# ScalarE's start reordered and PE's warm-up cut from seven products to five in a hybrid decoder step

## What is computed

```
for l in range(DEPTH):
    hn = rmsnorm(xp, norm_mix[l])
    q_nope, q_rope, c_kv, k_r, qb, kb, vb, g = project_in(hn, pos_p, w_in[l], ...)
    a_out, b_out, c_out = MLA, dilated-window attention, conformer convolution
    xp = xp + concat[a_out, b_out, c_out] @ w_out[l]
    xp = xp + peer(rmsnorm(xp, norm_ffn[l]), ...)      # top-16 product-key retrieval over 16384 experts
    ... the same for the 8 sample tokens, with their caches
y = rmsnorm(x, norm_final)
```

## Time and profile before

| what | value |
|---|---|
| median of 3 runs (lowest to highest) | 2046.28 us (2045.88 to 2046.68) |
| the profiled execution's own time | 2044.14 us |
| its span, first to last instruction | 2042.3 us |
| PE busy | 2016.6 us (99%) |
| PEld, DVE, ACT, POOL busy | 88%, 76%, 63%, 6% |
| mean granted TensorE clock | 0.998 |
| first product of the first chunk (L940) starts | 14.97 us |

### The profile page before, as it was taken

How to read it: one execution, slowest core, us unless ns; L and a number is a source line. 1 busy time by engine, 2 the same in 40 slices (tenths; PEclk the granted TensorE clock), 3 DMA queues, 4 the chain that set the end, 5 groups by cost and what they waited for, 6 DMA issues and landing times. The chain is left out here.

```text
span 2042.3 us, 40772 instructions
## 1 busy us (share of the span) xinstructions
PE 2016.6 (99%) x15562; PEld 1796.2 (88%) x15562; DVE 1550.3 (76%) x3543; ACT 1290.1 (63%) x2567; POOL 123.2 (6%) x140
## 2 busy tenths in 40 slices
PE   9999999999999999999999999999999999999998
PEld 7876999999999888788887779999999998887887
DVE  6846699868899776676678467989589997765766
ACT  5466455668888656565564654565688886555654
POOL 2200000000000100100022000000000001001000
PEclk9999999999999999999999999999999999999999
DMA  9454367776666898898763642777766669988886
GB/s 331 143 174 165 125 202 255 244 249 218 212 221 212 294 318 292 296 325 272 242 231 143 214 158 91 241 252 252 237 217 223 211 219 309 312 281 296 271 267 219
DMA packets 137376, 481.76 MB, mean 236 GB/s; under 512 B 25666, under 2 KB 42082, under 8 KB 130768
## 3 DMA queue, kind: packets, MB, share of 16 engines
q1 hardware_dynamic: 124640, 438.45, 64.2%
q0 software_dynamic: 10496, 40.42, 5.6%
q10 hardware_dynamic: 2048, 0.30, 0.1%
HBM read 475.83 MB, written 104.21 MB: 284 GB/s over the span
## 5 line engine op out<-in xcount | busy, mean ns | idle before, releaser
L2235 DVE TENSOR_TENSOR parts<-region,parts 128x1024 fp32r<-128x1024 f32 x512 | 625.6, 1222 | 300.1 <-ACT parts L1563 297.9
L1239 PE MATMUL ps<-tokens_hi,parts 128*128 128x256 f32 x4096 | 760.5, 284 | 0.0
L1563 ACT CAST parts<-region 128x1024 fp32r<-128x1024 f32 x512 | 538.8, 1052 | 270.5 <-PE ps L1286 202.4
L1286 PE MATMUL ps<-parts,parts_hw 128*128 128x512 f32 x3024 | 688.7, 390 | 0.0
L1286 PEld LDWEIGHTS ps<-parts,parts_hw 128*128 128x128 f32 x3024 | 567.0, 188 | 123.8 <-DVE parts_hw L2285 6.9
L1239 PEld LDWEIGHTS ps<-tokens_hi,parts 128*128 128x128 f32 x4096 | 637.0, 188 | 0.9 <-issue 0.4
L1239 PE MATMUL ps<-parts_hw,parts 128*128 128x256 f32 x2048 | 574.1, 280 | 0.0
L1239 PEld LDWEIGHTS ps<-parts_hw,parts 128*128 128x128 f32 x2048 | 386.7, 189 | 0.0
L1609 ACT ACTIVATE big<-ps 128x256 f32<-128x256 f32 (+31 forms) x252 | 131.7, 522 | 146.8 <-PE ps L1239 146.8
L1597 ACT CAST parts_hw<-big 128x256 fp32r<-128x256 f32 x256 | 171.4, 670 | 0.7 <-DVE big L2296 0.7
L1590 ACT ACTIVATE region<-region 128x128 f16<-128x128 f16 x512 | 169.3, 436 | 0.0
(11 more groups left out here) (329 smaller groups left out, 2199.5 us busy)
## 6 DMA issues: line engine op xcount, KB each, us to landing
region<-in_peer_uT SPq DMA_DIRECT2D x256, 512.0 KB, 4.0
region<-in_peer_v SPq DMA_DIRECT2D x256, 512.0 KB, 4.8
out<-in_state_win_k SPq DMA_DIRECT2D x112, 384.0 KB, 4.9
out<-in_state_win_v SPq DMA_DIRECT2D x112, 384.0 KB, 4.9
big<-in_window_keysT SPq DMA_DIRECT2D x16, 576.0 KB, 5.3
big<-in_state_win_v SPq DMA_DIRECT2D x48, 192.0 KB, 4.0
region<-in_w_out SPq DMA_DIRECT2D x4, 2048.0 KB, 8.9
big<-in_peer_wq SPq DMA_DIRECT2D x4, 2048.0 KB, 11.4
```

What stands on the lines that cost most here:

```text
L1239: mm = pe.matmul(ps[:, j % ZB, 0:SEQ], a, hp[b][:, c, :], start=(c == 0 and n == 0), stop=(c == KD - 1 and n == 2))
L1286: mm = pe.matmul(ps[:, 2 * half + t, :], w_t[a][:, 128 * t:128 * t + 128], v_t[b][:, 512 * half:512 * half + 512], start=(j == 0 and n == ...
L1563: act.copy(hi_t[n % HIGHS], rows_t[n % ROWS]).then_inc(high[l], 1)
L2235: dve.tensor_tensor(lo_t[n % ROWS], rows_t[n % ROWS], hi_t[n % HIGHS], ALU.subtract).then_inc(low[l], 1)
```

## The change

ACT's six constant DMAs move from behind the `norm_mix` gains to behind the three roots of the first norm; the table load and its throwaway root thereby follow the gains directly. WARM goes from 7 to 5. Nothing else changes; no wait is added or taken away.

```
-WARM = 7
+WARM = 5
...
-            act.dma_start(iota[:, :], C["iota"]).then_inc(consts_ld, 16)
...
-            act.dma_start(wmask[:, :], C["wmask"]).then_inc(consts_ld, 16)
             act.wait_ge(ones_set, 1)
             act.activation(stat[:, 15:16], stat[:, 15:16], ACT.Sqrt)
...
                     root(0, MIX, 1)
+                    act.dma_start(iota[:, :], C["iota"]).then_inc(consts_ld, 16)
...
+                    act.dma_start(wmask[:, :], C["wmask"]).then_inc(consts_ld, 16)
```

More of the change, by code:

```diff
@@ L1358, in _ @@
                 act.dma_start(g_mix, L("norm_mix", 0).rearrange("(k p) -> p k", p=P)).then_inc(gm_ld[0], 16)
[L1359 to L1364, removed]
             act.wait_ge(ones_set, 1)
@@ L1378, in _ @@
                     root(0, MIX, 1)
+                    act.dma_start(iota[:, :], C["iota"]).then_inc(consts_ld, 16)
+                    act.dma_start(pages[:, :], A["page_rows"]).then_inc(consts_ld, 16)
+                    act.dma_start(sub[:, :], C["sub"]).then_inc(consts_ld, 16)
+                    act.dma_start(rope[:, :, :], C["rope"]).then_inc(consts_ld, 16)
+                    act.dma_start(bmask[:, :], C["bmask"]).then_inc(consts_ld, 16)
+                    act.dma_start(wmask[:, :], C["wmask"]).then_inc(consts_ld, 16)
                 def input_high(c, k):
```

## The result

The changed kernel takes 2051.13 us (median of 9 runs, 2049.97 to 2053.05) against 2046.27 for the kernel before (9 runs beside it). It is slower by 4.86 us: ratio 1.0025, 95% interval 1.0017 to 1.0034. The forecast was 2045.1, with 2047.6 as the upper end. The sign was wrong, and the time lies outside the range.

The account below looks back on a forecast made before the run. PE, busy 99% of the span, was taken to be the bound, so its start mattered: L902 at 18.7 instead of 19.90, set by the constants landing at 14.6, gains 1.2 us: 2046.28 - 1.2 = 2045.1, range 2043.6 to 2047.6.

Parts of the forecast that it names:

- The table and the roots: ACT and DVE start: table load at 1.65, reciprocal 2.39 us earlier, from the second square on DVE 1.71 us earlier.
- Two products fewer: PE warm-up: four fast passes of 0.43 go, 1.72 us; PE is free to transpose at 9.52 instead of 11.24.
- The six issues in their new place: ACT behind the third root: issues take 3.50 us, first eviction at 11.95, costing 0.44 of the 1.72 gained.
- The rival that ACT is held in its issues: ACT's issues held up like SP's `q_norm`: first eviction about 14.5, 1.3 us later, 2047.6; chance 0.06.
- When the constants land: PE's wait before the first L940: `iota` lands near 10.75, five more at 0.77 each, the last at 14.6.
- the sum: Eviction chain lets L902 go at 18.62, PE's own way at 18.7: 1.2 us earlier, median 2045.1.
- The rule that was weighed there: DMA engines take turns among queue rows with work; constants would pass w_in's backlog, a gain of 1.2 us.
- The rival: Constants land late, PE waits before the first L940: 2048.5, or 2050.2 with the clock; chance 0.09, a fifth with clock.
- its threshold of 16.0: Landing of the constants at which nothing is left of the gain: 15.9 + 4.02 is L902's old 19.90.
- the forecast's four signs of being wrong: `wmask` after 16; an ACTq issue of 2 us or more; clock falling before 20 us; later PE wait growing by the gain.
- the forecast's comparison: PE's idling from 13.07 to 14.7 is shorter than the 1.8 us it sat through before.

Follow-up runs that it names:

- the kernel with the second chunk held back: Changed kernel, but SP issues the eight pieces of w_in's second chunk only behind the third root: 2048.31 against 2046.10 for before (ratio 1.0007).
- POOL's first: First constant in the changed kernel with POOL issuing the six constants from its own queue instead of ACT: 2044.77 against 2046.10 for before (ratio 0.9990).
- both experiments that idled for 2.9 us or more: Changed kernel with a warm-up of seven, 2051.41; changed kernel with SP issuing w_in's second chunk only behind the third root, 2048.31.
- the one that was taken apart: Changed kernel, 2051.13; against it, 16 idle products on PE ahead of the wait for the constants gave 2048.31.
- the kernel with the wait at its use: Changed kernel, but PE waits for the six constants in layer 0's second norm, not before the first chunk: 2043.53 against 2045.92; repeated, 2044.70 against 2045.84.

## Why the prediction was wrong

**The table and the roots: right.** Third root at 8.25 (forecast 8.35), second square at 6.98 and released by X (forecast 7.1).

**Two products fewer: right in kind, and hidden in this execution.** The first transpose began at 10.68, not at 9.52, because the clock rose later than in the execution before: loads of PEld in the changed kernel take 0.33 us as late as 8.52 and 0.20 from 9.38, where the earlier trace rows has 0.34 at 6.68 and 0.19 at 7.38.

```profile
8.52 0.33 PEld L915 LDWEIGHTS ps<-ident,ones 128*128 128x128 f32 x1 [0.52 <-issue]
...
9.38 0.20 PEld L915 LDWEIGHTS ps<-ident,ones 128*128 128x128 f32 x1 [0.52 <-issue]
```

The forecast took the clock's rise of one execution for that of all. It costs up to 1.2 us here and decided nothing.

**The six issues in their new place: too dear.** They took 2.86 us (8.26 to 11.12), not 3.50, and began beside the third root. ACT was free before its first eviction. The rival that ACT is held in its issues fell.

**When the constants land: this step failed.** It took `ident`'s 2.3 us for the first constant, because ACT's queue would be empty by then, and added 0.77 for each of the others. The second part held nearly: 14.26 to 18.46 is 0.84 each. The first part was 6.0 in place of 2.3, and that 3.7 us is nearly all of the 3.86 by which `wmask` came later than the forecast 14.6. L902, forecast at 18.7, came 5.86 later: 3.84 for the first L940 at 18.54 in place of 14.7, and 2.0 for the clock, for which the sum had no term. Rows of the same hours pointed the other way. In the earlier trace rows the pieces of w_in took 6.2; those are the first chunk's, issued up to about 6 us. The second chunk's, which SP issued from there to 10.4 and so beside the constants' new place, took still longer in the kernel before:

```profile
big<-in_w_in SPq DMA_DIRECT2D x8, 256.0 KB, 7.2
```

A constant issued on ACT's queue at 8 us joins SP's backlog, though its own queue is empty, as the kernel with the second chunk held back shows; and POOL's first, with nothing ahead of it on its queue from 1.32 us on, took 5.5. In the kernel before, `iota`'s 5.9 could be read in two ways, as a line behind the `norm_mix` gains or as the backlog of everything; the forecast chose the first because the landings were even, and evenness does not tell the two apart.

The rule that was weighed there, the Trainium skill's ("DMA: Bandwidth & Descriptors", section Queues, rings and completion order) on taking turns among queue rows, was read as if a new row were served at once. The trace shows that it was not: `iota` took 6.0 on an otherwise empty queue, and for 3.5 us of them its row moved no packet.

**The rival was the outcome.** The prediction priced late constants at 2048.5, and 2050.2 with the clock; measured 2051.13. The landing, 18.5, lies past its threshold of 16.0, and two of the forecast's four signs of being wrong came: `wmask` after 16 and a fallen clock before 20 us. What was wrong was its chance, 0.09 with a fifth of that for the clock. The clock fell in the profiles of both executions of the changed kernel, and of both experiments that idled for 2.9 us or more (in these two about 1 us behind the idling); the forecast's comparison, 1.8 us of idling without a fall, did not cover 4.3.

The advice of the Trainium skill ("DMA: Bandwidth & Descriptors", section Rules for kernel authors) to issue early and wait late is what the experiments bear out from both ends: issuing early from POOL (2044.77) or waiting late on PE (2043.53 and 2044.70) each takes the whole loss away, and most likely leaves a small gain.

## What to carry to other kernels

Before moving a DMA issue to a later hour, read what transfers issued at that hour take to land, on any queue, and not what one took on an idle chip or what its own queue holds. Look for every wait that counts on it: here six small constants shared one semaphore, and PE waited for all of them some 190 us before it read the first. A wait of a few us on TensorE early in a kernel is to be priced with the clock that falls in it or just behind it, here 1.3 to 2.0 us in four profiles, 1.96 on top of 2.70 in the one that was taken apart.

## What was not expected of the hardware

The clock rises at another hour in each execution. In the kernel with the wait at its use PEld's loads are fast from 6.39 on, in that kernel's second profile from 9.04, in the changed kernel from 9.38, with the same five products from 3.1 to 3.3 us (the rows are of the first):

```profile
5.90 0.25 PEld L915 LDWEIGHTS ps<-ident,ones 128*128 128x128 f32 x1 [0.52 <-issue]
6.39 0.19 PEld L915 LDWEIGHTS ps<-ident,ones 128*128 128x128 f32 x1 [0.24 <-issue]
```

In the middle of one layer or both, 0.4 to 3.3 us behind the start of L1137 (16 products of 6 columns) and without PE idling, the granted clock halves in each of the twelve profiles, for 3.4 to 10.3 us. The kernel with five warm-up products alone, as fast as the kernel before in its median, had two long ones (windows of its trace):

```profile
172.80:183.00 10.20, 10.20 (x41) 7.98 (x42) 7.81 (x18) 5.06 (x11) 0.00 (x0) 0.50 0.82 315
...
1186.60:1196.80 10.20, 10.20 (x45) 8.08 (x45) 6.75 (x17) 5.89 (x12) 0.00 (x0) 0.50 0.92 349
```

Such stretches account for the 3.4 us by which the spans of the changed kernel and the kernel before differ beyond the 4.66: the lag is 6.75 behind the stretch in the first layer and 8.06 behind that in the second. Part of their cost is hidden: the longest wait of the earlier trace rows, L1166's 1.4 to 1.8 us for DVE, stands in every layer with no such stretch or one of 3.4 us, and in none with a longer one, where PE, being slower, comes later than DVE. They may be behind the scatter of some 5 us among runs of one kernel (before, in one session: 2043.76 to 2048.90). What sets their length was not tried. It also stays open why a constant's first packet waits behind SP's transfers; the runs show that it does, and that it waits ahead of its first packet.
